# One transformer block pair on one core: order of side work in three stages, and the grouping of the scan's loads

## The reference

```python
kk = heads(k * k_k)
kk = kk * lax.rsqrt(jnp.maximum(jnp.sum(kk * kk, axis=-1, keepdims=True), 1e-24))
b_h = kk * a_h

def step(S, inp):                       # rwkv7_scan, once forwards and once in reverse
    r_t, w_t, k_t, v_t, kk_t, b_t = inp
    sa = jnp.einsum('bhij,bhj->bhi', S, -kk_t)
    S = (S * w_t[:, :, None, :] + sa[..., None] * b_t[:, :, None, :]
         + v_t[..., None] * k_t[:, :, None, :])
    return S, jnp.einsum('bhij,bhj->bhi', S, r_t)

mod = c_act @ ada_w[i] + ada_b[i]       # the six shift, scale and gate vectors
```

## Time and profile before

| | PE | PEld | DVE | ACT | POOL |
|---|---|---|---|---|---|
| busy us | 2919.2 | 2379.8 | 1467.3 | 1153.6 | 280.4 |
| share of the span | 93% | 76% | 47% | 37% | 9% |

### The profile page before, as it was taken

The page is one execution under the profiler, slowest core; times in us unless marked ns, Lnnn a source line. Parts: engine busy times, 40 slices in busy tenths (PEclk is TensorE's granted clock), DMA queues, the critical chain, the costliest instruction groups (busy, mean ns, idle before and its releaser), DMA issues.

```text
span 3128.4 us, 56667 instructions
## 1 busy us (share of the span) xinstructions
PE 2919.2 (93%) x25024; PEld 2379.8 (76%) x25024; DVE 1467.3 (47%) x2046; ACT 1153.6 (37%) x1897; POOL 280.4 (9%) x318
## 2 busy tenths in 40 slices
PE   6986799699997899999999999999999999999997
PEld 5675677588884578888888887787887888888886
DVE  3668667245454364333343326665436533244323
ACT  5665565222223243322332225533234333243322
POOL 1000023444441100000000000000000000000000
PEclk8996899799997799999999999999999999999998
DMA  3320234211100222222222222222222222223222
GB/s 136 124 73 3 84 131 161 66 38 38 38 13 30 101 88 94 88 95 101 95 90 94 98 96 94 88 92 91 94 95 92 95 96 95 94 95 125 97 94 81
DMA packets 100565, 273.07 MB, mean 87 GB/s; under 512 B 9248, under 2 KB 36512, under 8 KB 100320
## 3 DMA queue, kind: packets, MB, share of 16 engines
q1 hardware_dynamic: 91536, 236.94, 22.0%
q0 software_dynamic: 8784, 32.51, 3.1%
HBM read 256.69 MB, written 12.58 MB: 86 GB/s over the span
## 4 chain that ended last, share of the span: by engine, by line
PE 62%; DVE 2%; ACT 1%; DMA 1%; issue 0%; DVEq 0%; ACTq 0%
PE be_ps L2924 45%; PE be_ps L2945 15%; DVE be_ring L2714 1%; PE be_ps L2958 1%; PE be_ps L2666 0%; PE be_ps L2660 0%; ACT be_whi L2991 0%; DVE be_raw_r L3097 0%; DMA be_raw<-in_w_out 0%; DMA be_raw<-in_ple_gate 0%; DVE be_total L2679 0%; DVE ext_r L2724 0%; ACT big L2997 0%; DVE big L2687 0%; DVE big L2696 0%
## 5 line engine op out<-in xcount | busy, mean ns | idle before, releaser
L3097 DVE TENSOR_TENSOR be_raw_r<-be_raw,be_whi 128x1024 fp32r<-128x1024 f32 x361 | 442.2, 1225 | 1005.9 <-ACT be_whi L2991 1005.8
L2924 PE MATMUL be_ps<-ext_r,be_whi 128*128 128x512 f32 x2304 | 714.3, 391 | 15.4 <-PEq L2334 8.6
L2991 ACT CAST be_whi<-be_raw 128x1024 fp32r<-128x1024 f32 x361 | 378.8, 1049 | 898.8 <-DMA be_raw<-in_ffn_down 317.2
L2924 PE MATMUL be_ps<-big_r,be_whi 128*128 128x512 f32 x2048 | 641.9, 394 | 2.4 <-DVE big_r L2722 2.4
L2924 PEld LDWEIGHTS be_ps<-ext_r,be_whi 128*128 128x128 f32 x2304 | 432.3, 188 | 108.7 <-issue 10.3
L2924 PEld LDWEIGHTS be_ps<-big_r,be_whi 128*128 128x128 f32 x2048 | 383.0, 188 | 97.5 <-DVE big_r L2722 3.1
L2924 PE MATMUL be_ps<-ext_r,be_raw_r 128*128 128x512 f32 x1152 | 449.4, 390 | 0.0
L2924 PE MATMUL be_ps<-big_r,be_raw_r 128*128 128x512 f32 x1024 | 407.9, 398 | 0.0
L2945 PE MATMUL be_ps<-ext_r,be_whi 128*128 128x512 f32 x1152 | 354.6, 389 | 0.0
L2924 PEld LDWEIGHTS be_ps<-ext_r,be_raw_r 128*128 128x128 f32 x1152 | 217.1, 188 | 45.4
L2945 PEld LDWEIGHTS be_ps<-ext_r,be_whi 128*128 128x128 f32 x1152 | 216.3, 188 | 44.9
(11 more groups left out here) (328 smaller groups left out, 3905.1 us busy)
## 6 DMA issues: line engine op xcount, KB each, us to landing
be_raw<-in_ffn_gate SPq DMA_DIRECT2D x88, 512.0 KB, 3.5
be_raw<-in_ffn_up SPq DMA_DIRECT2D x88, 512.0 KB, 3.5
be_raw<-in_ffn_down SPq DMA_DIRECT2D x88, 512.0 KB, 3.5
be_raw<-in_conv_in SPq DMA_DIRECT2D x48, 512.0 KB, 3.5
gp_ada<-in_ada POOLq DMA_DIRECT2D x24, 512.0 KB, 3.7
rp_ada<-in_ada POOLq DMA_DIRECT2D x24, 512.0 KB, 3.9
rwkv_prepared<-big SPq DMA_DIRECT2D x16, 512.0 KB, 3.2
be_raw<-in_w_out SPq DMA_DIRECT2D x16, 512.0 KB, 3.5
```

The costliest lines, as they stand in the source:

```text
L2924: mm = pe.matmul(ps[:, bank], part[:, k * P:(k + 1) * P], xs(k), start=(k == 0 and i == 0), stop=(k == KD - 1 and i == 2))
L2991: act.copy(w.hi[:, n % 3], w.raw[:, n % 3]).then_inc(w.hi_ready, 1)
L3097: dve.tensor_tensor(w.lo(n), w.raw[:, n % 3], w.hi[:, n % 3].bitcast(F32), ALU.subtract).then_inc(w.lo_ready, 1)
```

## The change

Five edits stand in the diff. In the GLA projection, `per_step` gives step 2 and step 7 two tiles in place of three, and steps 10 and 11 three in place of two. In the RWKV projection, the fourth accumulation comes ahead of the reciprocal. In the RWKV mixing, a turn's input is loaded with two DMAs of 384 KB, one for each direction, that wait only for POOL's use of the buffer, and the count that ACT waits for changes with it. And on ACT the copy to `nv` moves from behind both copies of `u` to between them, while on PE `front_nv` moves from behind `products(0)` to behind `products(1)`.

```diff
-        modulation = Modulation(core, ctx, "gp", dram_ada, c, mod, 0, (3, 3, 3, 2, 2, 2, 2, 3, 0, 0, 2, 2))
+        modulation = Modulation(core, ctx, "gp", dram_ada, c, mod, 0, (3, 3, 2, 2, 2, 2, 2, 2, 0, 0, 3, 3))
...
                 if s == 8:
+                    accumulate(3)
                     dve.wait_ge(kk_rooted, 1)
                     dve.reciprocal(kk_scale, kk_scale).then_inc(kk_scaled, 1)
-                    accumulate(3)
...
                 for d in two:
-                    for k in (0, 2, 4):
-                        if t >= 4:
-                            sp.wait_ge(*pe_made.by(("xx1", "xx2", "xx3", "xx4", "u0", "u1")[3 * d + k // 2], t - 4))
-                        sp.dma_start(fed[t // 2 % 2][:, t % 2, d, k:k + 2],
-                                     prepared[:, g, 2 * d + k:2 * d + k + 2, tokens(d, j)]).then_inc(fed_loaded[t % 4], 16)
+                    sp.dma_start(fed[t // 2 % 2][:, t % 2, d], prepared[:, g, 2 * d:2 * d + 6, tokens(d, j)]
+                                 ).then_inc(fed_loaded[t % 4], 16)
...
-                act.wait_ge(fed_loaded[t % 4], t // 4 * 96 + 96)
+                act.wait_ge(fed_loaded[t % 4], t // 4 * 32 + 32)
...
-                if ahead:
-                    nv_out(t + 1, dve_made.by("rhs1", t))
+                    if m == 0 and ahead:
+                        nv_out(t + 1, dve_made.by("rhs1", t))
...
-                    if m == 0 and ahead:
+                    if m and ahead:
                         front_nv(t + 1, 1 - par)
```

## The result

The kernel after takes 3144.1 us (median; 3138.0 to 3152.8), beside 3125.6 us of the kernel before on the same chip. The ratio is 1.0053, 95% interval [1.0036, 1.0070], so it is slower by 16.6 us, between 11 and 22 (the two medians are 18.5 apart). I had said 3167 us, 37 us more than the execution that I worked from, and a range that began at 3147. The direction and most mechanisms were right; one term, the clock in the mixing, was not, and it is the largest part of the miss.

The account below looks back on a forecast made before the run. PE was taken to bound the RWKV projection and the mixing's turns. Terms -2.0 + 4.5 + 0 + 19.2 + 15 = +36.7 us on 3130.2 gave 3167 us, with an 8-in-10 range of 3147 to 3193.

Parts of the forecast that it names:

- The clock in the mixing: RWKV mixing: new PE gaps make three more turns fall to half clock, 5.0 us each, +15 us, between 0 and 65.
- GLA projection: Moved third tiles of steps 2 and 7: DVE's tail ends the stage near 219.1, -2.0 us, bounds 0 and -11.8.
- RWKV projection: Later reciprocal: PE idles 2.8 us and loses 1.7 at half clock, +4.5 us, between 2.8 and 6.2.
- Loads: Merged input loads of the mixing: same bytes and pieces, nobody waits for them, 0 us, from -1 to +12.
- `front_nv` and `nv`: Mixing's chunk steps: second state 1.31 us later, 0.03 gained in the first step, 15 turns, +19.2 us, bounds 11 and 36.
- rival A: Mixing: the clock holds as it does now, only the other terms count, +21.7 us, 3152; chance 0.25.
- the forecast: Whole kernel: the summed terms with a few more slow turns in the mixing, 3167 us, own range 3157 to 3178; chance 0.45.
- Rival B: Mixing: the clock falls in ten more turns, 50 us, giving 3202; chance 0.12.
- C: Mixing: bursts of loads delay PE's code, 12 us on top of the forecast, 3179; chance 0.07.
- D: Mixing: the delay is regained within the turn, 0.2 us a turn is left, 3136; chance 0.07.
- E: Mixing: `front_nv` held up the first state by 1.11 us and the second step hides it, -16.7 us, 3116; chance 0.04.

Follow-up runs that it names:

- edit 2: Part of the change: in the RWKV projection the fourth accumulation comes ahead of the reciprocal. Alone in the kernel before: 3138.8 us, ratio 1.0032.
- edit 4: Part of the change: `front_nv` behind `products(1)` on PE, copy to `nv` between the two copies of `u` on ACT. Undone in the kernel after: 3124.7 us, ratio 1.0008.
- edit 4 alone: Kernel before with only the moves of `front_nv` on PE and of the copy to `nv` on ACT: 3137.5 us, ratio 1.0044.
- the reciprocal's wait filled: Kernel after, with 11 overwritten 128x512 products on PE in its wait for the RWKV projection's reciprocal: 3140.4 us, ratio 1.0027.
- the gap of 1.0 us: Kernel after, with two more ACT copies into a spare tile ahead of its first copy of `u`: 3154.6 us, ratio 1.0078.
- the gap of 2.1 us: Kernel after, with six more ACT copies into a spare tile ahead of its first copy of `u`: 3186.6 us, ratio 1.0178.
- the two halves: Kernel before with only `front_nv` moved on PE: 3127.0 us, ratio 1.0012; with only the copy to `nv` moved on ACT: 3124.9 us, ratio 1.0002.

## Why the prediction was wrong

**The step that failed is "The clock in the mixing", +15 us.** I argued that the new gaps make some more turns fall and priced each fall at 5 us. The runs show about nothing in its place: the executions' mean clock is that of before (0.9579 beside 0.9567 to 0.9585, with 0.001 for edit 2), and the number of falls and their price were both wrong.

The number: ahead of the last turn there were 3.4, 0 and 10.2 us at half clock in the 14 turns of the three kernels with edit 4 in full and gaps as it leaves them (after, edit 4 alone, the reciprocal's wait filled), and 23.9, 0, 13.7, 10.2, 6.8, 10.2 in six whose steps are timed as before. So the new gaps of 0.6 and 0.7 us add nothing to the half clock that these traces can show. The price: a fall in the kernels with wider gaps lasts 3.4 us, or 6.8, and the turn takes 0.9 to 2.7 us more (25.55 - 23.4 = 2.1 in after), where the two of before lasted 10.2 and 13.7 us.

What the rows held was another thing than a step's gap. The idle time in their first piece is a single wait of PE in the middle of a group of like products in the levels. It is labelled "issue", as no other engine ended it; the fall of 647 us follows it, as that of 855 us follows one of 1.20:

```profile
645.56 0.94 PE L2016 MATMUL rw_ps<-rw_mx,rw_xt 64*64 64x32 f32 x25 [1.08 <-issue]
854.59 1.23 PE L2016 MATMUL rw_ps<-rw_mx,rw_xt 64*64 64x32 f32 x29 [1.20 <-issue]
```

In the six kernels timed as before all seven falls start within 3 us of the beginning of such a wait, of 0.79 to 1.20 us, and so does the one fall in after (1.01 us). Not each of these waits is followed by a fall: in the six kernels there are 13 of 0.78 us or more, one of them of 1.47 us, and six pass without one. So the falls that I counted belong to an irregular wait, and some 1 us of the 4.9 to 5.9 us that I took as a fall's price is the wait itself. The new gap has a part in some falls all the same. The two falls with the reciprocal's wait filled start 0.1 and 0.8 us behind the beginning of the gap of 0.62 us. With the gap of 1.0 us four of five falls follow it, and with 2.1 us all but one do.

Stretches at half clock in before (columns as above):

```profile
647.20:657.20 10.00, 10.00 (x193) 9.97 (x190) 4.24 (x8) 1.02 (x4) 2.54 (x2) 0.50 0.10 28
855.40:868.90 13.50, 13.50 (x274) 13.48 (x274) 5.77 (x10) 2.57 (x9) 3.64 (x4) 0.50 0.12 33
```

I took one profile's two falls as what a kernel has and what falls cost; that profile held more half clock than any of the other five, and the clock of one kernel's executions goes from 0.951 to 0.961. I also added everything to its 3130.2 us, and before's median came out at 3125.6 with more runs; without the clock's 15 us the sum on that base is 3147. The sign of the idea was not wrong: in the series of gaps the clock is lower at 1.0 us and clearly so at 2.1 us. The rule of the Trainium skill that I quoted (TensorE: Matmul & The Clock Gate, A second HAM failure mode: psum-queue depth-cycling) is borne out at the gap of 2.1 us, where nearly each turn falls, and not at 0.6 to 0.7 us, where a whole trace ran its 14 turns at a clock of 1.00.

**The others, one by one.** GLA projection: -2.0 forecast, -3.8 measured; DVE does end the stage, but the last tile came 2.3 us sooner than my chain of loads had it. RWKV projection: +4.5 forecast, +5.8 measured; the wait was right to 0.01 us, and the low clock lasted twice as long as behind the wait in the back end. Loads: 0, and nothing that can be seen beside it, within some 4 us; at the start ACT waits 4.78 us for its first loads, where it waited 4.79. `front_nv` and `nv`: 1.31 a turn forecast for the second step, 1.27 measured, and the mechanism, ACT's order, is shown by the two halves apart; the first step gave 0.11, not 0.03. So 15 x 1.16 = +17.4, for 19.2. Sum of the measured terms: -3.8 + 5.8 + 17.4 = +19.4 us with nothing for the clock, and the time shows +16.6, 11 to 22. That is nearest to rival A, whose 3152 was 21.7 us over before; I had given the forecast 0.45 and it 0.25. Rival B has no slow turns to show for it. For C I look at PE's waits labelled "issue" in those 14 turns: 1.8 to 6.6 us in eight kernels with the merged loads, 1.2 to 8.4 in six without, so nothing of 12 us. D fails, as the ordinary turn kept 1.15 of the 1.16 us, and E fails, as the first step held only 0.11 us.

**What stays open.** Where the steps are as in before, a fall lasted 3.4 to 13.7 us, four of seven 10 or more; with the later `u` 3.4 or 6.8, though behind a fall PE is busy without a break in before and after, as the rows at clock 0.50 show. No run says why. Nor does one say what PE waits for in the middle of a group, the wait labelled "issue". And the mean over the kernels of those 14 turns, 321.7 us without edit 4 (six) and 332.7 with it (three), differs by 11 us where 14 x 1.16 is 16; less time at half clock accounts for about half of the missing 5, and fewer waits labelled "issue" (3.3 us beside 5.1 on average) for some 2.

## What to carry to other kernels

Before a copy is put ahead of another in an engine's queue, ask when its source is ready in the new order: either move here was free or cheap alone, and 14 to 17 us only as a pair. Price a clock that falls now and then from several profiles, and from the mean clock of all executions; one profile's slow turns are luck, good or bad. Look at what PE waited for just ahead of a fall before you lay the fall to a gap. The wait among dense products here cost its own length and as much again for the clock (2.8 and 3.0 us), and filling it with products gave the second part back.

## What the runs showed of the hardware

- A wait of 2.8 us among dense products of 128x512 was followed by 6.7 us at the lower of the two clock levels (1.2 GHz) in all traces with edit 2 and no filler; with 11 products in the wait there was none.
- Gaps of 0.6 and 0.7 us in each turn left the clock at 2.4 GHz for 329 us on end (edit 4 alone); one of 2.1 us a turn cost 1.6 us a turn on top of itself, with a mean clock of 0.9477 where 0.6 us has 0.9579.
- The clock differs between executions of one kernel: 0.951 to 0.961 in 76 executions of before, and the longer ones are by and large those with the lower clock.
- In six kernels all seven falls among the small products follow a wait of PE of 0.8 to 1.2 us in the middle of a group of products, labelled "issue"; 13 such waits stand in their traces.
- Where a timeline names "issue" as the end of an idle stretch, as for the 2.81 us here, the real reason can be a semaphore wait: the same products read "DVE" with fillers ahead of them.
